# Transformer layer on one core: half of the first modulation job ahead of step 6, and two row units moved behind the fourth job

## The reference

```python
c_act = silu(c)
sh1, sc1, gt1, sh2, sc2, gt2 = split(c_act @ w_ada + b_ada, 6)
h = rms_norm(x, g_mix) * (1 + sc1) + sh1
rq, rk, rv, rg, aq, ak, av = split(h @ w_in + b_in)
mix = concat([retention(rq, rk, rv, rg), window_attention(aq, ak, av, sinks)]) @ w_out
x = x + gt1 * mix
h = rms_norm(x, g_ffn) * (1 + sc2) + sh2
x = x + gt2 * conv_glu(h, w_up, w_conv, b_conv, w_down)
y = rms_norm(x, g_final) * (1 + f_scale) + f_shift
```

## Time and profile before

| | us |
|---|---|
| median of 3 runs | 1213.98 (1213.51 to 1214.6) |
| the profiled execution | 1214.47 |
| its span | 1212.8 |
| TensorE busy in the span | 1176.8 |
| mean granted clock, of full speed | 0.987 |

### The profile page before, as it was taken

One profiled execution on the slowest core, in us unless ns is written; L12 is line 12 of the kernel. 1 busy time (PEld: TensorE's weight loads), 2 busy tenths in 40 slices (PEclk: granted clock), 3 DMA queues, 4 the chain that ended last, 5 costly groups with the idle time before them and its releaser, 6 DMA issues.

```text
span 1212.8 us, 19627 instructions
## 1 busy us (share of the span) xinstructions
PE 1176.8 (97%) x6800; PEld 986.7 (81%) x6800; DVE 898.7 (74%) x1111; ACT 655.9 (54%) x947; POOL 180.0 (15%) x307
## 2 busy tenths in 40 slices
PE   5899999999999999999999999999999999999995
PEld 3677889777888788888888888888888877888784
DVE  3346658898789787887887887877655666897886
ACT  5333335552845448565565665656655555555652
POOL 6343312121211110010111011000000000120101
PEclk9899999999999999999999999999999999999998
DMA  9999999998788984888887878885565557897841
GB/s 305 377 368 392 367 357 401 350 406 324 279 287 327 333 301 156 298 285 282 282 286 275 290 271 289 279 281 186 180 201 176 196 184 280 286 357 256 311 176 69
DMA packets 167478, 342.73 MB, mean 283 GB/s; under 512 B 10266, under 2 KB 103552, under 8 KB 166784
## 3 DMA queue, kind: packets, MB, share of 16 engines
q1 hardware_dynamic: 129072, 206.13, 49.0%
q0 software_dynamic: 37536, 134.30, 29.6%
q10 hardware_dynamic: 816, 1.58, 0.4%
HBM read 339.87 MB, written 2.10 MB: 282 GB/s over the span
## 4 chain that ended last, share of the span: by engine, by line
PE 86%; DMA 6%; DVE 3%; issue 2%; ACT 1%; POOL 1%; DVEq 0%; ACTq 0%; POOLq 0%
PE ps L1575 27%; PE ps L1580 14%; PE ps L1551 14%; PE ps L1553 13%; PE ps L1552 13%; DMA ada_raw<-in_w_ada 3%; DMA arena<-in_w_ada 2%; PE ps L1680 2%; DMA raw<-in_w_in 1%; DVE xb L1349 1%; POOL ada_raw L543 1%; DVE arena L1347 0%; PE ps L1857 0%; PE ps L1956 0%; ACT whi L659 0%
## 5 line engine op out<-in xcount | busy, mean ns | idle before, releaser
L666 ACT ACTIVATE whi<-raw 128x1024 fp32r<-128x1024 f32 x256 | 271.6, 1062 | 286.5 <-PE ps L1580 180.6
L1020 DVE TENSOR_TENSOR wlo<-raw,whi 128x1024 fp32r<-128x1024 f32 x256 | 311.9, 1222 | 104.0 <-ACT whi L666 104.0
L1575 PE MATMUL ps<-hh,whi 128*128 128x512 f32 x1408 | 353.0, 392 | 0.1
L1575 PEld LDWEIGHTS ps<-hh,whi 128*128 128x128 f32 x1408 | 253.2, 189 | 45.7 <-issue 0.4
L1551 PE MATMUL ps<-whi,hh 128*128 128x512 f32 x608 | 242.4, 399 | 1.3 <-DVE arena L1125 1.0
L1553 PE MATMUL ps<-whi,hh 128*128 128x512 f32 x608 | 237.7, 391 | 0.0
L1552 PE MATMUL ps<-wlo,hh 128*128 128x512 f32 x608 | 237.3, 390 | 0.0
L1025 DVE SCALAR_TENSOR_TENSOR acc<-ada_raw,c_act,acc 128x1024 f32<-128x1024 f32 (+1 forms) x176 | 225.1, 1279 | 14.1 <-DMA ada_raw<-in_w_ada 13.5
L659 ACT ACTIVATE whi<-raw 128x1024 fp32r<-128x1024 f32 x124 | 130.2, 1058 | 190.1 <-PE ps L1553 173.1
L1580 PEld LDWEIGHTS ps<-hh,wlo 128*128 128x128 f32 x1408 | 192.1, 190 | 13.7
L1580 PE MATMUL ps<-hh,wlo 128*128 128x256 f32 x1408 | 196.3, 282 | 0.0
(11 more groups left out here) (161 smaller groups left out, 818.9 us busy)
## 6 DMA issues: line engine op xcount, KB each, us to landing
raw<-in_w_up SPq DMA_DIRECT2D x176, 512.0 KB, 4.4
ada_raw<-in_w_ada POOLq DMA_DIRECT2D x140, 512.0 KB, 7.0
raw<-in_w_down SPq DMA_DIRECT2D x44, 1024.0 KB, 6.8
ada_raw<-in_w_final_ada POOLq DMA_DIRECT2D x64, 512.0 KB, 5.3
arena<-in_w_ada POOLq DMA_DIRECT2D x52, 512.0 KB, 9.0
raw<-in_w_in SPq DMA_DIRECT2D x52, 512.0 KB, 9.9
raw<-in_w_in SPq DMA_DIRECT2D x16, 1024.0 KB, 8.6
raw<-in_w_out SPq DMA_DIRECT2D x16, 1024.0 KB, 6.9
```

The source lines that it names most:

```text
L666: nc.scalar.activation(whi[:, i % RING, :], raw_of(step0 + i), ACT.Copy).then_inc(hi_ready, 1)
L1020: nc.vector.tensor_tensor(wlo[:, i % RING, :], raw_of(step0 + i), whi[:, i % RING, :], ALU.subtract).then_inc(lo_ready, 1)
L1575: nc.tensor.matmul(bank_of(m), whi[:, slot, tile(m, j)], hh[:, k0 + j, :, :].rearrange("p i s -> p (i s)"), start=start and j == 0, stop=F ...
```

## The change

There are three edits. In the table of units, the two that ran behind steps 35 and 37 (units 7 and 8) now run behind steps 38 and 39, and the units behind them are packed so that the order of units stays and from step 42 on nothing differs: 7 on step 38, 8 and 9 on 39, 10 on 40, 11 and 12 on 41. On ScalarE, `first_heads(1, 0)` and the modulation of stage 1 come ahead of `hi(6)`. On VectorE, `first_rows(1)`, `mod_cols` and the two `h_lo` of stage 1 come ahead of `lo(6)`.

```diff
-UNIT_STEPS = ((19, 20, 23, 24), (31, 32, 34, 35, 37), range(38, 48), (49, 51, 53, 54), range(55, 66), (66, 66, 67, 67, 68, 69),
+UNIT_STEPS = ((19, 20, 23, 24), (31, 32, 34), (38, 39, 39, 40, 41, 41), range(42, 48), (49, 51, 53, 54), range(55, 66), (66, 66, 67, 67, 68, 69),
...
             hi_group(0, 1, 5)
             first_heads(0, 0)
-            hi_group(0, 5, 7)
+            hi(5)
             first_heads(1, 0)
             stage_in(1)
-            hi_group(0, 7, 13)
+            hi_group(0, 6, 13)
...
             first_heads(0)
             lo(5)
-            lo(6)
             first_rows(1)
             mod_cols(0, FIRST_BANKS[1], 0, 1)
             for k in STAGE_K[1]:
                 h_lo(k, 0)
+            lo(6)
             lo(7)
             lo(8)
```

## The result

The median of five runs is 1220.74 us (1219.36 to 1223.34) against 1213.51 for the kernel before, run beside it (five runs): ratio 1.0066, 95% interval 1.0047 to 1.0085. The change makes the kernel slower by 0.5 to 0.9%. The forecast was 1.9 us faster, with a range up to 1216.3.

The account below looks back on a forecast made before the run. TensorE, busy 97% of the span, was taken to bound the kernel, so only its waits and half clock could be won. 0.5 + 2.8 - 1.4 = 1.9 us gained: median 1212.1 us, range 1209.2 to 1216.3.

Parts of the forecast that it names:

- The first term: Around 50 us, first_rows(1) ahead of lo(6): 5.5 us local gain, of which loads leave 0.5 (0 to 1.8).
- my own sign of being wrong: Prediction wrong if the lead at 127 us exceeds 2 us, or the burst lands in over 8 or under 6 us.
- The second term: Sums of job 3, near 173 us: 1.14 us of idle and 1.7 lost to half clock go, 2.8 us gained.
- The third term: Steps 41 and 42: unit 9's load and the burst behind it come late, TensorE stalls 1.4 us (0 to 5.6).
- The steps behind 42 still fit: After step 42: VectorE, some 3 us behind, catches up where it idled before, so no further loss was counted.
- the rival of the late burst: Unit 9's load, issued only after unit 7, stalls step 40 by 5.6 us: 1216.3, or 1218.0 with half clock; chance 0.17.
- the old burst: Loads of pair 0 of job 4, units 10 and 11 at 179.99 before; first landed after 3.7 us, third 7.3.
- The half clock did not move: Rival: idle at the sums of job 2 (126.77) grows, a 1.7 us half-clock loss follows: 1213.8 us; chance 0.11.

Follow-up runs that it names:

- the cut loads of units 0 to 3: First half alone, with the loads of units 0 to 3 cut to 64 of 1024 columns, part of the second modulation left out: 1213.6 us, one run.
- second half alone: Kernel before plus only the new table of units, first_rows(1) still behind lo(6): 1221.14 us against 1213.50, ratio 1.0058.
- first half alone: Kernel before plus only the edits to ScalarE and VectorE, old table of units: 1211.52 us against 1213.50, ratio 0.999.
- unit 7 at 36: Kernel before plus the ScalarE and VectorE edits, unit 7 moved only to step 36, unit 8 to 38: 1209.47 us against 1213.84, ratio 0.9975.
- only unit 8 moved: Changed kernel, but unit 7 stays behind step 35 and unit 8 goes to 38: 1211.67 us against 1213.50, ratio 0.9989.
- VectorE's part alone: First half alone, but ScalarE keeps its order from before, so only VectorE's edit remains: 1210.71 us, one run.
- the order with unit 9 last: Changed kernel, but GpSimd issues pair 0 of job 4 and units 10 and 11 ahead of unit 9: 1218.71 us against 1213.50, ratio 1.0048.

## Why the prediction was wrong

**The first term, 0.5 us, is not refuted.** The idle and the half clock at 50 us went as worked out: pair (1, 1) at 55.2 for the 55.1 that 61.7 - 5.5 - 1.06 gives. That the loads then decide was right too, as the cut loads of units 0 to 3 show. The lead at the sums of job 2, read against the one trace of before, is 2.2 to 2.6 us, more than the 1.8 that I allowed, and above 2 us was my own sign of being wrong. But against the trace of the second half alone it is 0.7 to 1.1 us. The times of the first half alone give 1.2 us by the ratio, 0 to 2.4, and 2.0 by the medians: 0.5 is inside, and the true gain may be a few times as large. The Trainium skill ("DMA: Bandwidth & Descriptors", section "Queues, rings and completion order") has each DMA engine take turns between the queues with work, packet by packet. The prediction read a term of 0 out of that; the times do not decide against 0 either.

**The second term, 2.8 us, was about right.** The first half alone and unit 7 at 36 differ by it (and by unit 8, which costs nothing that shows): from the sums of job 2 to those of job 3 46.0 and 45.0 us, and the clock from 170 to 180 us 0.83 and 1.00. The medians differ by 2.0 us (each by its own runs), the spans by 1.5. The half clock was not there in every execution: with unit 7 still at step 35, the traces of the kernel with only unit 8 moved and of that with VectorE's part alone have idles of 0.56 and 0.53 us there and a clock of 1.00, so in them only half a microsecond was to be won.

**The third term, the stall of 1.4 us, is what failed, and in it the sentence "The steps behind 42 still fit".** The place and the cause were right: the rival of the late burst names unit 9's load behind unit 7. Its price and its follow-ups were not. Between the changed kernel and unit 7 at 36, both with the first two terms, the medians differ by 11 us, where the prediction has 1.4. That the way is unit 9's load is shown by the kernel that frees only that load: with the same units on the same steps the loss is gone. By the trace of the changed kernel: waits of 2.57, 2.21 and 1.44 us, 6.2 together, and stretches at half clock of 3.4 and 6.8 us (0.83 from 190 to 200; 0.74 and 0.92 from 210 to 230), which lose another 5.1. Together 11.3.

- The wait at step 41: predicted 0.7 and 0.9 at step 42, measured 2.57 and none. I gave the burst the latencies of the old burst and one load more: unit 9's load took 5.2 us where that gave 3.7, and unit 10's 9.28 where it gave 7.1.
- Pair 1 of job 4: not in the sum at all, because of "The steps behind 42 still fit". I wrote that VectorE catches up where it idled before, but in the kernel before it had only one pause from 181.6 to 200.3 us, the 1.02 us of the earlier trace rows. After, it has no pause from 190.7 to 207.4 us. Late as it stays, it frees the buffers late, and in GpSimd's one order pair 1 stands behind them (1.4 us of lateness by the estimate above), at a time when the path has to make up for what it did not move from 170 to 180 (206 instead of 347 GB/s, 1.4 MB, 3.6 us at 389): that is the larger part.
- In the changed kernel the large waits on TensorE each had a stretch at half clock behind them. I gave that only to the rival. It is not there in every execution: the second half alone waited 2.42 us for lo(41) and had a clock of 1.00 from 190 to 210 us.

The stretch of the kernel before in which VectorE was to catch up; its third pair of numbers is VectorE's:

```profile
190.00:200.00 10.00, 10.00 (x86) 10.00 (x85) 10.00 (x9) 4.36 (x7) 2.11 (x4) 1.00 1.04 401
```

**The rivals.** The late burst came, with 5.7 us as the stall that would take it over the 0.2%; the waits were 6.2 us, by a way that I had not seen. The half clock did not move to the sums of job 2, which have no idle now.

**What stays open:** the size of the first half's gain between 0 and 2.4 us; why the same wait is followed by half clock in one execution and not in another; and why the order with unit 9 last, whose waits add to 3.5 us, is as slow as 1218.7 in its median when its profiled execution took 1216.

## What to carry to other kernels

When a consumer is moved later, list the loads that wait for its buffer, and everything issued behind them in the same order; price the move by when those loads are needed, not by when the consumer is. Where the load path is near its limit, 10 us in which one queue can issue nothing are owed back later. Before a lead is read from two single traces, look at a third whose instructions are the same up to that point. To get work out of the way of an urgent step, move it just behind that step, as unit 7 to step 36.

## What the runs showed of the hardware

The half clock does not follow from the length of an idle by itself. 1.14 us (before) and 0.93 us (first half alone) of idle ahead of the sums of job 3 had a stretch of 3.4 us behind them; 0.56 us in the kernel with only unit 8 moved had none (clock 1.00 from 170 to 180), and neither had 0.88 us ahead of the sums of job 1 (before and second half alone, clock 1.00 from 80 to 90), nor 1.05 us at 238.71 in the kernel before (clock 1.00 from 230 to 250). In the changed kernel the wait of 2.57 us had a stretch of 3.4 us behind it, in the second half alone the wait of 2.42 us had none. Waits close together had twice the stretch in the changed kernel (2.21 and 1.44 us, 6.8 us) and none in the kernel with the loads of units 12 to 15 cut (1.04 and 0.88 us).

A load of 0.52 MB issued by GpSimd took 3.7 us from issue to landing at the head of the burst at 179.99 before, 5.2 us at the head of the burst at 179.86 after, 9.28 us as the fourth of that burst, and 12.0 us as the second row of pair 1.
